# Output products by token block, with squares in front of an attention's end, a feed-forward tile by block, and half a head in front of block 1's transposes

## The reference

```
# block one
y = concat([rmsnorm(ya, ga), rmsnorm(yb, gb), rmsnorm(yc, gc)])   # three attentions
x = x + y @ w_o
x = x + cross(rmsnorm(x, norm_cross), rmsnorm(mem, norm_mem), w_cq, w_ckv, w_co)
h = rmsnorm(x, norm_ffn)
gate, up = split(h @ w_gu)
x = x + (silu(gate) * up) @ w_down
# block two, layers 0 and 1
x = x + g1 * mixer(rmsnorm(x) * (1 + sc1) + sh1)      # layer 0: gating and pooling
x = x + g2 * peer(rmsnorm(x) * (1 + sc2) + sh2)       # layer 1: differential attention, o @ w_out
```

## Time and profile before

| | before |
|---|---|
| median of 3 runs | 2407.14 us (2404.5 to 2407.78) |
| profiled execution, its own time | 2407.42 us |
| its span on the core | 2405.5 us |
| PE busy | 2332.8 us (97%) |
| DVE busy | 1826.1 us (76%) |
| ACT busy | 1031.8 us (43%) |
| POOL busy | 298.9 us (12%) |
| DMA | 430.11 MB, mean 179 GB/s |
| chain that ended last | PE 79%, DVE 14%, DMA 3%, ACT 2% |

### The profile page before, as it was taken

The page is one execution under the profiler, slowest core; times in us unless marked ns, Lnnn a source line. Parts: engine busy times, 40 slices in busy tenths (PEclk is TensorE's granted clock), DMA queues, the critical chain, the costliest instruction groups (busy, mean ns, idle before and its releaser), DMA issues.

```text
span 2405.5 us, 36432 instructions
## 1 busy us (share of the span) xinstructions
PE 2332.8 (97%) x12984; PEld 1987.6 (83%) x12984; DVE 1826.1 (76%) x3786; ACT 1031.8 (43%) x1580; POOL 298.9 (12%) x228
## 2 busy tenths in 40 slices
PE   8998999999999999999999998999999999999998
PEld 7776998679887888888888777798977888888887
DVE  5465887869998777777777766699987777777777
ACT  4453332232334444444444446423434444444444
POOL 0000000036680000000000000265800000000000
PEclk9999999999999999999999999999999999999999
DMA  7424888954216566666565551232155666666563
GB/s 268 159 76 161 302 324 331 371 222 141 79 36 200 168 192 190 188 191 191 191 190 188 200 197 36 105 126 86 44 175 175 190 188 191 191 191 190 188 190 130
DMA packets 97734, 430.11 MB, mean 179 GB/s; under 512 B 11232, under 2 KB 11872, under 8 KB 90720
## 3 DMA queue, kind: packets, MB, share of 16 engines
q1 hardware_dynamic: 97632, 428.75, 53.0%
HBM read 427.66 MB, written 1.05 MB: 178 GB/s over the span
## 4 chain that ended last, share of the span: by engine, by line
PE 79%; DVE 14%; DMA 3%; ACT 2%; issue 1%; SPq 0%; DVEq 0%; ACTq 0%; PEldq 0%
PE ps L516 44%; PE ps L892 15%; PE ps L895 8%; PE ps L848 4%; DVE HN L1962 4%; DVE HN L1960 3%; DMA arena<-in_ada 1%; DMA ring<-in_stream 1%; PE ps L668 1%; PE ps L633 1%; DVE arena L1642 1%; PE ps L561 1%; PE ps L689 1%; DVE ring_rounded L1520 1%; PE ps L575 1%
## 5 line engine op out<-in xcount | busy, mean ns | idle before, releaser
L516 PE MATMUL ps<-ring_rounded 128*128 128x512 f32 x3072 | 742.5, 392 | 8.4 <-DVE ring_rounded L1980 7.9
L1980 DVE TENSOR_TENSOR ring_rounded<-ring,ring_rounded 128x1024 fp32r<-128x1024 f32 (+1 forms) x688 | 652.6, 960 | 128.0 <-ACT ring_rounded L1337 104.8
L516 PEld LDWEIGHTS ps<-ring_rounded 128*128 128x128 f32 x3072 | 560.6, 188 | 127.7 <-issue 15.5
L892 PE MATMUL ps<-HNHT_rounded,ring_rounded 128*128 128x512 f32 x1632 | 403.3, 389 | 0.0
L892 PEld LDWEIGHTS ps<-HNHT_rounded,ring_rounded 128*128 128x128 f32 x1632 | 306.2, 188 | 63.4
L1343 ACT ACTIVATE ring_rounded<-ring 128x1024 fp32r<-128x1024 f32 x202 | 214.3, 1061 | 237.1 <-PE ps L516 237.1
L516 PE MATMUL ps<-parts 128*128 128x256 f32 (+2 forms) x1248 | 269.7, 306 | 2.3 <-DVE parts L1515 1.7
L895 PEld LDWEIGHTS ps<-HNHT_rounded,ring_rounded 128*128 128x128 f32 x1632 | 222.6, 190 | 15.9
L895 PE MATMUL ps<-HNHT_rounded,ring_rounded 128*128 128x256 f32 x1632 | 227.6, 282 | 0.0
L1334 ACT ACTIVATE ring<-ps 128x256 f32<-128x256 f32 x204 | 78.3, 384 | 336.0 <-PE ps L895 336.0
L516 PEld LDWEIGHTS ps<-parts 128*128 128x128 f32 x1248 | 204.0, 189 | 15.5 <-DVE parts L1515 2.2
(11 more groups left out here) (270 smaller groups left out, 2860.5 us busy)
## 6 DMA issues: line engine op xcount, KB each, us to landing
ring<-in_experts_u SPq DMA_DIRECT2D x256, 512.0 KB, 3.5
ring<-in_experts_v SPq DMA_DIRECT2D x256, 512.0 KB, 3.5
ring<-in_stream SPq DMA_DIRECT2D x45, 2048.0 KB, 8.8
arena<-in_ada SPq DMA_DIRECT2D x96, 512.0 KB, 7.2
arena<-in_keys SPq DMA_DIRECT2D x2, 1024.0 KB, 15.6
ring<-in_stream SPq DMA_DIRECT2D x1, 1792.0 KB, 7.4
ring<-in_stream SPq DMA_DIRECT2D x1, 1664.0 KB, 8.1
ring<-in_stream SPq DMA_DIRECT2D x1, 1040.0 KB, 19.0
```

The source lines that it names most:

```text
L516: mm = pe.matmul(out_, p, q, start=(first and i == 0), stop=(last and i == 2))
L892: pe.matmul(r3(t, 2), exp_uh[:, j % 2, c], ht_both[:, :, k, :], start=(k == 0), stop=False)
L1980: return dve.tensor_tensor(dst, src, h.bitcast(F32), ALU.subtract)
```

## The change

Five edits that go together:

1. **Tiles by token block.** `rows_pair` makes (0,0), (1,0), (0,1), (1,1), so that both halves of block 0 are done after two tiles. Block 1 is no longer transposed before the first tile but inside one (`turns`): after three k-tiles of (0,0) in "wo", after three of (1,0) in "odo". The splits on ACT and DVE are put in the order in which the tiles need them. In "odo" tile (0,1) becomes plain: `pair_parts` gives None for i = 0.
2. **Early squares.** In "wo" ACT squares the results of the first four attention units during the attention (`y_square`) and has only the last two behind it. In "odo" DVE scales block 0 behind unit 6 and multiplies its gain behind unit 7, before the bound of block 1.
3. **wco and the feed-forward's start.** Block 0 of "ffn" is transposed inside the last tile of "wco"; tile 0 of ("gu", 0) is plain and by block, so that only columns 256 on of that chunk are split. DVE's low part of ("gu", 1) moves behind `split_ht`, and two modulations go from here to two turns of the loop, with their fetches.
4. **Half a head first.** `turned_by_block` (wcq and the mixer) and `plain_queries` (both layers) do half of tile 1 for block 0 in front of block 1's transposes instead of behind them.
5. Fillers: those of ("ffn", 1) and ("gu", 0) go, ("sub", 0) has 6 instead of 18.

```diff
-FILLERS = {("y", 0): 11, ("ffn", 1): 8, ("mix_0", 0): 18, ("sub", 0): 18,
-           "mix_1": 20, ("gu", 0): 6, ("probs", 0): 6, ("probs", 6): 6, ("probs", 8): 9, ("values", 15): 5}
+FILLERS = {("y", 0): 11, ("mix_0", 0): 18, ("sub", 0): 6,
+           "mix_1": 20, ("probs", 0): 6, ("probs", 6): 6, ("probs", 8): 9, ("values", 15): 5}
...
-BLOCKS_BEHIND = {("wcq",): 3, ("gu", 0): 6, ("gu", 1): 5, ("ev", 0): 3, ("ev", 1): 3, ("pool",): 11, ("evs",): 9, ("evo", 1): 14}
+BLOCKS_BEHIND = {("wcq",): 3, ("gu", 0): 6, ("gu", 1): 3, ("ev", 0): 3, ("ev", 1): 3, ("pool",): 11, ("evs",): 9, ("evo", 1): 14}
 BLOCKS_BEHIND |= {name: 3 for name in [("gu", i) for i in range(3, 11)] + [("down", i) for i in range(6)]}
+BLOCKS_BEHIND |= {("gu", 5): 4, ("gu", 6): 4}
...
-        PAIRS = {"wo": ("y", 3648, 7744), "odo": ("sub", 1312, 9504)}
+        PAIRS = {"wo": ("y", 3648, 7744), "odo": ("sub", None, None)}
...
+            if i == 0 and high_0 is None:
+                return None
...
-            def rows_pair(stage, ready=lambda b, k: None):
+            def rows_pair(stage, turns):
...
+                for i, b in ((0, 0), (1, 0), (0, 1), (1, 1)):
+                    if b == 0:
+                        wait_weights(pe, (stage, i))
                     t = claim(((stage, i), b))
-                    if b != i:
-                        pe.wait_ge(sem("pair_ht"), NB * at_ + i + 1)
-                    high, low_ = pair_parts(stage, i)
+                    w = r3(weights((stage, i)), KT)
+                    in_two = None if (i, b) == (0, 0) else pair_parts(stage, i)
+                    if in_two is not None:
+                        pe.wait_ge(sem("pair_ht"), NB * at_ + b + 1)
                     c = slice(b * P, (b + 1) * P)
                     for k in range(KT):
-                        if b != i and k % 4 == 0:
-                            pe.wait_ge(sem("pair_low"), 4 * at_ + 2 * i + k // 4 + 1)
-                        if i == 1:
-                            ready(b, k)
-                        mm = in_parts(t, [h[:, k, c] for h in ht_parts], (high[:, k, :], low_[:, k, :]), k == 0, k == KT - 1)
+                        if (i, b, k) in turns:
+                            turn_block(*turns[(i, b, k)])
+                        if in_two is None:
+                            if k % 4 == 0:
+                                wait_drained(pe, (norm_, b, k))
+                            mm = pe.matmul(t, HT[:, k, c], w[:, k, :], start=(k == 0), stop=(k == KT - 1))
+                        else:
+                            if b != i and k % 4 == 0:
+                                pe.wait_ge(sem(f"pair_low_{i}"), 2 * at_ + k // 4 + 1)
+                            mm = in_parts(t, [h[:, k, c] for h in ht_parts], [w_[:, k, :] for w_ in in_two], k == 0, k == KT - 1)
                     released[(stage, i)] = publish(mm, ((stage, i), b))
 
...
+                turned_block(t[1], chunk, (name, 1), parts_of[1], 0, [0])
                 turn_block(norm, 1)
-                turned_block(t[1], chunk, (name, 1), parts_of[1], 0)
...
             attention(ATT["self"])
-            turn("y")
-            rows_pair("wo", first_turn("cross"))
+            turn_block("y", 0)
+            rows_pair("wo", {(0, 0, 3): ("y", 1), (1, 1, 4): ("cross", 0)})
...
+                        if (b, half, k) == (1, 1, 2):
+                            turn_block("ffn", 0)
...
                     released[("wco",)] = publish(mm, ("wco", b, half))
-            turn("ffn")
-            for i in range(FT // 2):
-                turned_in_parts(("gu", i), ht_ready=HT_PARTS["ffn"] - 4 if i == 0 else None)
+            wait_weights(pe, ("gu", 0))
+            t = claim((("gu", 0), 0))
+            w = r3(weights(("gu", 0)), KT)[:, :, 0:256]
+            turned_block(t, ("gu", 0), (("gu", 0), 0), w, 0, norm="ffn")
+            turn_block("ffn", 1)
+            turned_block(t, ("gu", 0), (("gu", 0), 0), w, 1, norm="ffn")
+            turned_in_parts(("gu", 0), HT_PARTS["ffn"] - 4, tiles=[1])
...
+                    turned_block(t[1], name, names[1], of_head[1], 0, [0])
                     turn_block(f"peer_{l}", 1)
-                    turned_block(t[1], name, names[1], of_head[1], 0, [0])
+                    turned_block(t[1], name, names[1], of_head[1], 0, [1])
...
-                act.activation(weights_high(name), weights(name)[:, 0:IN_PARTS_SIZE[name]], ACT.Copy).then_inc(sem("weights_high"), 1)
-
-            def pair_highs(stage):
...
-                norm_ = PAIRS[stage][0]
...
+                dst, src = weights_high(name), weights(name)[:, 0:IN_PARTS_SIZE[name]]
+                if name == ("gu", 0):
+                    dst, src = r3(dst, KT)[:, :, 256:], r3(src, KT)[:, :, 256:]
...
+            def pair_high(stage, i, half):
+
+                k = slice(4 * half, 4 * half + 4)
+                wait_weights(act, (stage, i))
+                act.activation(pair_parts(stage, i)[0][:, k], r3(weights((stage, i)), KT)[:, k], ACT.Copy).then_inc(sem(f"pair_high_{i}"), 1)
+
+            def pair_tokens_high(stage, b):
+
+                for i in (0, 4):
+                    wait_drained(act, (PAIRS[stage][0], b, i))
+                c = slice(b * P, (b + 1) * P)
+                act.activation(ht_parts[0][:, :, c], HT[:, :, c], ACT.Copy).then_inc(sem("pair_ht_high"), 1)
...
+
+            def y_square(u):
+
+                i, b = u["no"] // NB, u["b"]
+                lo, hi = y["segs"][i]
+                wait_drained(act, ("o", u["no"]))
+                c = y["col"] + 3 * b + i
+                step(act.activation(HN[:, b, lo:hi], ymix[:, b, lo:hi], ACT.Square, accum_out=ss[:, c:c + 1]))
+
+            attention(ATT["self"], lambda i: y_square(ATT["self"][i - 2]) if i >= 2 else None)
             load_table(ACT.Sqrt)
+            for b in range(NB):
+                y_square(ATT["self"][4 + b])
+                settle()
+                c = y["col"] + 3 * b
+                step(act.activation(rms[:, c:c + 1], ss[:, c:c + 1], ACT.Sqrt, bias=eps, scale=1.0 / 512))
+                act.activation(rms[:, c + 1:c + 3], ss[:, c + 1:c + 3], ACT.Sqrt, bias=eps, scale=1.0 / 256).then_inc(sem("rooted"), 1)
             act.wait_ge(sem("y_ready"), 1)
-            root("y")
-            pair_highs("wo")
+            pair_high("wo", 0, 0)
+            pair_tokens_high("wo", 0)
+            act.wait_ge(sem("normed"), NB * y["no"] + NB)
+            pair_high("wo", 1, 0)
+            pair_high("wo", 1, 1)
+            pair_high("wo", 0, 1)
+            pair_tokens_high("wo", 1)
...
             load_table(ACT.Sqrt)
             sub_root(0)
+            wait_tile(act, ("s", ATT["diff"][-1]["no"], 1))
+            pair_high("odo", 1, 0)
+            pair_high("odo", 1, 1)
+            pair_tokens_high("odo", 0)
             sub_squares(1)
             sub_root(1)
-            pair_highs("odo")
...
-                dve.tensor_tensor(weights_low(name), weights(name)[:, 0:IN_PARTS_SIZE[name]], weights_high(name).bitcast(F32), ALU.subtract).then_inc(sem("weights_low"), 1)
+                dst, src, high = weights_low(name), weights(name)[:, 0:IN_PARTS_SIZE[name]], weights_high(name)
+                if name == ("gu", 0):
+                    dst, src, high = [r3(a, KT)[:, :, 256:] for a in (dst, src, high)]
...
+            def pair_low(stage, i, half):
+
+                k = slice(4 * half, 4 * half + 4)
+                high, low_ = pair_parts(stage, i)
+                dve.wait_ge(sem(f"pair_high_{i}"), 2 * PAIR_NO[stage] + half + 1)
+                dve.tensor_tensor(low_[:, k], r3(weights((stage, i)), KT)[:, k], high[:, k].bitcast(F32), ALU.subtract).then_inc(sem(f"pair_low_{i}"), 1)
+
+            def pair_tokens_low(stage, b):
+
+                c = slice(b * P, (b + 1) * P)
+                dve.wait_ge(sem("pair_ht_high"), NB * PAIR_NO[stage] + b + 1)
+                dve.tensor_tensor(ht_parts[1][:, :, c], HT[:, :, c], ht_parts[0][:, :, c].bitcast(F32), ALU.subtract).then_inc(sem("pair_ht"), 1)
...
-            scale("y")
-            gain("y", HT, col("out_norm"))
-            pair_lows("wo", True)
-            add_to_x([((b, i), (("wo", i), b)) for i in range(2) for b in range(NB)], second=lambda: pair_lows("wo", False), norm="cross",
+            scale_block("y", 0)
+            gain_block("y", 0, HT, col("out_norm"))
+            scale_block("y", 1)
+            pair_tokens_low("wo", 0)
+            gain_block("y", 1, HT, col("out_norm"))
+            gained("y")
+            pair_low("wo", 1, 0)
+            pair_low("wo", 1, 1)
+            pair_tokens_low("wo", 1)
+            pair_low("wo", 0, 0)
+            pair_low("wo", 0, 1)
+            add_to_x([((b, i), (("wo", i), b)) for b in range(NB) for i in range(2)], norm="cross",
                      first=lambda: gain_block("cross", 0, HT, col("norm_cross")))
             scale("cross", [1])
...
             modulation(3)
```

(39 more changed lines are left out.)

70 lines of the change are left out of this document (15 added, 55 removed).

## The result

| | before | after |
|---|---|---|
| median | 2405.48 us (2404.06 to 2407.78, 6 runs) | 2386.14 us (2384.53 to 2390.31, 6 runs) |
| ratio, after to before | | 0.9923, 95% interval 0.9912 to 0.9934 |
| profiled execution, its own time | 2407.42 us | 2384.53 us |
| its span | 2405.5 us | 2382.7 us |
| PE busy | 2332.8 us | 2319.9 us |

The change made the kernel faster by 19.3 us (0.8%), where 14.2 were forecast. Two things are in these 6.9: 1.7 because the three runs shown of before had a median of 2407.14, and six have 2405.48; 5.1 because the measured gain is larger than the sum.

What follows compares the result with a forecast made beforehand. The prediction took PE, busy 97% of the span, as the bound. Terms −3.2 (wo, wcq), −1.9 (cross attention), −5.7 (wco, first chunk), +1.9 (mixer), +0.2 (plain queries), −5.5 (odo) sum to −14.2: 2393 us, range 2387.5 to 2399.5.

Steps and rivals of the forecast that it cites:

- Faster: Whole kernel: the change makes it faster, chance 0.91.
- the base: Whole kernel before: profiled 2407.42 us, taken as 0.3 above the median; the forecast gain was subtracted from it.
- 7.0 + 1.1: wo's first product onward: a plain tile 7.0 us plus block 1's transposes inside it 1.1; similar units in odo.
- I take −0.9 of these 2.1: Cross attention: values and transposes lose 2.1 us to the lower clock; an earlier start saves 0.9, bounds 0 and −2.1.
- wcq: wcq: a half tile in front of block 1's transposes covers the idle 0.56, −0.4 us.
- as taken (−1.0): Cross attention: DVE starts earlier because its low part is halved, −1.0 us, bounds 0 and −1.5.
- Block 0 loses two narrower ones: wo: fewer squares behind attention, with the root's table loading overlapped, bring the transposes of y 1.7 us earlier.
- wco and the first chunk: wco to the first feed-forward chunk's release: −5.7 us, bounds −6.3 and −3.5; low part and modulations delayed DVE's additions.
- The mixer: Mixer: half a head in front of block 1's transposes delays the pool matrix fetch and what follows, +1.9 us.
- Odo's early norm: odo: block 0's norm starts behind unit 6's weighing, so the transposes begin 4.2 us earlier; odo in all −5.5.
- The plain queries: Plain queries, two places: block 1's transposes come half a head later, +0.2 us for both, between −0.5 and +1.0.
- The loop of the feed-forward: Feed-forward loop: two moved modulations cost DVE 1.15 to 1.2 each, within 1.70 idle per turn; rival slower, chance 0.03.

Runs made afterwards that it cites:

- Experiment 6: Kernel before with more fillers in the idle times in front of the transposes of y, the cross attention's probabilities and sub: 2401.08 us, ratio 0.9982.
- Experiment 5: Changed kernel with one more unused DVE operation, 2.3 us, in front of the cross attention: 2389.85 us, ratio 0.9938.
- experiment 9: Kernel before, with ACT's squares and roots of norm y waiting for their own block's last weighed unit, not DVE's signal behind all attention: 2402.6 us, ratio 0.9988.
- experiments 7: Changed kernel with all six squares of norm y behind the attention: 2388.11 us, ratio 0.9925.
- 8: Changed kernel with DVE's low part of the feed-forward's second chunk back in front of the additions of wco's tiles: 2389.02 us, ratio 0.993.
- experiment 12: Changed kernel with block 1's transposes of norm ffn in front of the feed-forward's first quarter instead of behind it: 2393.53 us, ratio 0.9955.

## Why the prediction was wrong

Faster was right, with chance 0.91, and the places were. Two steps of the sum failed, both too small to the same side, and the base was 1.7 high. The first failed step is the units of PE: "7.0 + 1.1" for a plain tile and the transposes inside it, 1.8 us too much in two places. The second is the clock in the cross attention: "I take −0.9 of these 2.1", where 1.83 came. With the base at 2405.48 the same sum gives 2391.3 and its range would have begun at 2385.8, below the measured 2386.14: the base alone would have brought the time inside, and so would the units; that three runs gave a high base was bad luck. The 5.1 beyond the sum are about 1.8 of units, 0.9 of the clock, 0.5 because the first products of wo and odo started earlier than laid out, 0.4 in the queries behind odo, 0.3 in wcq, and 1.3 outside of the places, where executions of one kernel differ by more; wco's term, 0.2 smaller than forecast, goes the other way.

**Units of PE.** The forecast had 26.2 us from the first product of wo to its end, measured 25.4; 27.7 in odo, measured 26.7. A plain tile followed by a tile in parts takes 6.5 from start to start, not 7.0, and transposes inside a tile 0.8 to 0.9, not 1.1, since the next row starts before a row's modelled end. The 14.00 and the 1.09 were lengths; lengths of rows overlap. That is 1.8 in two places. Both paths were laid out at full speed, so what the lower clock had cost there before is in these two forecasts already, also where the text counted only 1.3 for it (in odo block 1's transposes at 1506.19 had also been slow).

**The clock in the cross attention.** The prediction took the lower clock for a matter of luck. The slow stretch was in both profiles of before at the same place and in neither of the changed kernel's; −0.99 came from DVE's earlier start, as taken (−1.0), and −1.83 from the clock. Experiment 6 shows the cost without any change to the data's way: the transposes come no earlier behind the scores (192.73 − 185.55 = 7.18, before 7.13), and the stretch is 1.79 shorter. Experiment 5 shows the reverse: 2.3 more on DVE and the stretch is slow again. At the three places together more fillers gave back 1.4, 1.8 and 2.5 in the profile, 5.7 in all, and 3.8 in the median; the median is the surer figure, and as large as a fifth of the 19.3.

**The Trainium skill's rule** ("TensorE: Matmul & The Clock Gate", What's actually happening), that the look at activity runs free of the program, was given as a reason why −0.9 could be 0 or −2.1. At the three places the runs show no such spread: two profiles of before agree in the clock to 0.02, and in experiment 9, whose waits in the cross attention and odo are as before, both were slow again (1.92 and 1.94 for eight transposes). Elsewhere the runs agree with the rule: behind one wait of 2.96 or 2.97 eleven of fourteen profiles were slow and three not, and behind one of 2.7 one profile of before was slow and the other not. Among the seven profiles of the changed kernel and its variants with waits of 0.9 to 1.5 from the cross attention to wco, wco's start was slow in two (experiments 7 and 8) and the cross attention's values in one (12, 0.58 from 192 to 196), without a change there. So the −1.83 was likely, not certain, and why the three places were slow each time stays open.

**wo: right number, wrong cause.** "Block 0 loses two narrower ones" was the reason for −1.7; 1.82 was measured, but with all squares late it is 1.54 still. What bound ACT was DVE's signal behind block 1's last unit (idle 1.80 <-DVEq in the earlier trace rows), for which block 0's squares waited too. The change drops that wait in passing, since `y_square` waits for the unit itself. Experiment 9 shows it in the kernel before. The row had named the releaser, and the prediction read it as the loading of a table.

**wco and the first chunk: right size (−5.47 for −5.7), half the reason wrong.** The prediction made the low part in front of the additions responsible for the addition at 216.66. Put back, it costs nothing. The quarter in front of block 1's transposes gives 4.6 (experiment 12). That block 0's transposes inside the last tile give the rest is argued, not shown.

**The mixer: right** (+1.79 for +1.9), and the old order gives it back. **Odo's early norm: right** (−4.34 for −4.2). **The plain queries**: +0.2 was forecast; behind odo it is −0.31: the wait of 1.22 in front of block 1's transposes goes, and one of 0.93 comes in front of the key scores. **The loop of the feed-forward** has its 1.70 idle on DVE as before, and from the release of chunk 0 to the mixer's transposes are 180.07 us after and 180.08 before: the two moved modulations and the moved low part cost nothing.

**Open.** Some 1 us of the 19.3 lies outside of the places (18.1 there). The draws of the clock in the long middle stretch are larger than that. Which execution is typical there, the runs can't say. The new order of tiles in wo and in odo, as such, has no run either.

**Best version.** The changed kernel with the mixer in the old order: 2385.36, ratio 0.9915, against 0.9923 and 0.9921 of the changed one. The trace shows 1.8 at its place in both pairs; the medians alone are within their intervals.

## What to carry to other kernels

A wait of PE costs itself and often, behind it, work at the lower clock. Whether that part is fixed or luck takes several profiles: two agreed at the three places, and two of before also agreed on the slow stretch near 1453, which three of the other profiles don't have. PE's own work is to be summed from start to start of its rows, and the base taken from as many runs as there are. Read a wait's releaser in the row to the letter and ask which signal stands behind it: one common signal for two blocks held block 0 back by 1.5 to 1.7 us, and letting go of it needed two other waits and no rearrangement. Filling a wait with the next block's product is worth it where there is a wait, and costs its own length where there is none and others depend on what it delays, as at the mixer.

## What the runs showed of the hardware

- At three places behind waits of 2.21, 2.07 and 1.77 us the granted clock fell in both profiles of the kernel before: 0.60 and 0.62 at 142, 0.51 and 0.51 at 194, 0.57 and 0.57 at 1504. Multiplications without use during the wait kept it at 1.00 in all three.
- A wait of 2 us and more is often, not always, followed by a slow stretch: behind 2.96 or 2.97 near 1440 to 1453 in eleven of fourteen profiles, behind 2.69 and 2.71 in one of the two profiles of before.
- Where PE had only waits of 0.9 to 1.5 us, from the cross attention to wco, the clock fell in three of seven profiles (0.76 from 199 to 206 in two, 0.58 from 192 to 196 in one), for 1.5 to 1.7 us. In the two with fillers in these waits it stayed at 1.00.
- Lengths of PE's rows overlap: the first tile of wo has rows of 2.81 + 4.46 = 7.27 us, but from start to start it takes 2.66 + 3.89 = 6.55; eight transposes inside a tile have 1.04 and move the next row by 0.87.
